# Two-layer hybrid trunk on one core: six more ring slots for the experts' weights, in memory that attention, caches, filter and retention no longer need

## The reference

```
for l in range(2):
    mod = silu(cond) @ w_ada[l] + b_ada[l]                  # six parts: sh1, sc1, g1, sh2, sc2, g2
    h = rms_norm(x, norm1) * (1 + sc1) + sh1
    qa, ka, va, hy, qr, kr, vr, gr = split(h @ w_in[l])
    ya = diff_attention(rope(qa), [k_cache, rope(ka)], [v_cache, va])   # caches and rope: latent group
    yb = hyena(hy)                                          # long convolution by FFT, implicit filter
    yc = rms_norm(retention(qr, kr, vr, s_cache)) * silu(gr)
    ga, gb, gc = split(sigmoid(h @ w_gate[l] + b_gate[l]))
    merged = ga*(ya @ w_branch_a) + gb*(yb @ w_branch_b) + gc*(yc @ w_branch_c)
    x = x + g1 * (merged @ w_out[l])
    h2 = rms_norm(x, norm2) * (1 + sc2) + sh2
    gate = top-2 of the experts of the top-1 group, by softmax(h2 @ w_router)     # 16 experts
    x = x + g2 * sum_e gate_e * ((silu(h2 @ w1_e) * (h2 @ w3_e)) @ w2_e)          # d_ff 512
y = rms_norm(x, final_g)            # and the context group's new keys, values, retention states
```

## Time and profile before

| | |
|---|---|
| median of the runs | 1264.77 us (3 runs, 1264.11 to 1270.05) |
| span of the profiled execution | 1267.2 us, 18560 instructions |
| TensorE matmul busy | 1228.1 us, 97% of the span, 7762 matmuls |
| TensorE weight load busy | 929.2 us (73%) |
| VectorE, ScalarE, GpSimd busy | 363.3 us (29%), 222.0 us (18%), 39.5 us (3%) |
| moved by the DMA engines | 362.06 MB, mean 286 GB/s over the span |
| chain that ended last | TensorE 86%, DMA 9% (experts' weights 7%, dense weights 2%) |
| mean granted clock of TensorE | 0.990 |

### The profile page before, as it was taken

How to read it: one execution, slowest core, us unless ns; L and a number is a source line. 1 busy time by engine, 2 the same in 40 slices (tenths; PEclk the granted TensorE clock), 3 DMA queues, 4 the chain that set the end, 5 groups by cost and what they waited for, 6 DMA issues and landing times.

```text
span 1267.2 us, 18560 instructions
## 1 busy us (share of the span) xinstructions
PE 1228.1 (97%) x7762; PEld 929.2 (73%) x7762; DVE 363.3 (29%) x917; ACT 222.0 (18%) x469; POOL 39.5 (3%) x80
## 2 busy tenths in 40 slices
PE   6999999999999999999999999999999999999996
PEld 5678888888897666666558888887888776666663
DVE  2441153134236111111233223423243611111113
ACT  2141013231030100111124101223202010000011
POOL 1001110000000000000000012000000000000000
PEclk9899999999989999999999999999999999999999
DMA  9779443424967999999976844343345599999992
GB/s 387 315 290 388 140 158 127 147 100 151 350 254 313 417 421 421 420 420 420 418 293 253 361 161 143 129 141 134 122 149 195 236 418 421 421 420 420 420 421 111
DMA packets 52601, 362.06 MB, mean 286 GB/s; under 512 B 6592, under 2 KB 6752, under 8 KB 9760
## 3 DMA queue, kind: packets, MB, share of 16 engines
q1 hardware_dynamic: 48672, 350.33, 69.3%
q0 software_dynamic: 3840, 10.47, 2.4%
HBM read 356.56 MB, written 2.64 MB: 283 GB/s over the span
## 4 chain that ended last, share of the span: by engine, by line
PE 86%; DMA 9%; DVE 2%; ACT 1%; issue 1%; SPq 0%; DVEq 0%; ACTq 0%
PE bank L713 24%; PE bank L1014 13%; PE bank L1050 9%; DMA ring<-in_experts 7%; PE bank L893 7%; PE bank L997 5%; PE bank L922 4%; PE bank L708 4%; PE bank L637 4%; PE bank L1092 3%; DMA ring<-in_weights 2%; PE bank L724 2%; PE bank L1029 1%; PE bank L973 1%; PE bank L697 1%
## 5 line engine op out<-in xcount | busy, mean ns | idle before, releaser
L713 PE MATMUL bank<-h,ring 128*128 128x256 f32 x1472 | 326.3, 380 | 0.0
L713 PEld LDWEIGHTS bank<-h,ring 128*128 128x128 f32 x1472 | 276.8, 190 | 40.9 <-issue 4.4
L1014 PE MATMUL bank<-ring,gates 128*64 128x256 f32 x2048 | 226.2, 380 | 8.0 <-DMA ring<-in_experts 4.3
L1014 PEld LDWEIGHTS bank<-ring,gates 128*64 128x64 f32 x2048 | 152.1, 137 | 79.7 <-issue 11.6
L1050 PE MATMUL bank<-ring,gates 128*64 128x512 f32 x512 | 113.4, 595 | 0.0
L1050 PEld LDWEIGHTS bank<-ring,gates 128*64 128x64 f32 x512 | 35.3, 137 | 66.7 <-issue 66.7
L997 PE MATMUL bank<-uc,gates 128*128 128x128 f32 x576 | 67.9, 276 | 0.1
L997 PEld LDWEIGHTS bank<-uc,gates 128*128 128x128 f32 x576 | 65.9, 192 | 0.7 <-DVE uc L1612 0.4
L1616 DVE SCALAR_TENSOR_TENSOR gates<-gates,bank 128x512 f32<-128x512 f32 (+1 forms) x18 | 11.8, 658 | 172.6 <-issue 161.3
L1092 PEld LDWEIGHTS bank<-gates,uc 128*128 128x128 f32 x256 | 47.3, 190 | 18.8 <-issue 13.0
L1092 PE MATMUL bank<-gates,uc 128*128 128x256 f32 x256 | 59.5, 386 | 0.0
(11 more groups left out here) (258 smaller groups left out, 1077.6 us busy)
## 6 DMA issues: line engine op xcount, KB each, us to landing
ring<-in_experts SPq DMA_DIRECT2D x204, 1024.0 KB, 11.7
ring<-in_weights SPq DMA_DIRECT2D x128, 1024.0 KB, 6.5
cst<-in_consts POOLq DMA_DIRECT2D x1, 1345.0 KB, 11.2
x<-in_x_in SPq DMA_DIRECT2D x1, 1024.0 KB, 5.0
sc<-in_s_cache POOLq DMA_DIRECT2D x2, 512.0 KB, 10.0
probs<-qk POOLq DMA_DIRECT2D x32, 32.0 KB, 3.0
va<-row_scratch POOLq DMA_DIRECT2D x2, 512.0 KB, 7.2
vr<-row_scratch POOLq DMA_DIRECT2D x2, 512.0 KB, 9.2
```

The source lines that it names most:

```text
L713: last = pe.matmul(bank[b][:, c * TOK:(c + 1) * TOK], w[:, k, c * P:(c + 1) * P], h[:, k, :], start=(k == 0), stop=(k == KT - 1))
L1014: last = pe.matmul(bank[b][64 * j:64 * j + 64, half * 256:half * 256 + 256], hgat[:, k, 64 * j:64 * j + 64], w[j][:, k, :], start=(k == 0) ...
```

## The change

Six slots, `lent`, are added for the experts' pieces alone, and thirteen tiles become views into them. `ring_table` now gives each piece the slot that has been free longest. It returns for each piece the count `USED` that `s_weights_used` must have reached. A lent slot counts as free from the end of the layer's last merge piece on. SyncE waits for `s_stores_read` once per layer, ahead of the experts. GpSimd's loads of layer 1's caches wait until TensorE has used the last piece of layer 0's experts. `rows_sb` moves to `arg`. By the new table the first six expert pieces of a layer wait for the end of the merge. Of those in the middle, each waits for the piece 14 places before. The first dense pieces of layer 1 wait for a count 11 below their own number (before: 7), and from the ninth on 7 again.

```diff
 SLOTS = 8
+LENT = 6
...
-    slot, count, filled = [], [], [0] * SLOTS
-    for n, piece in enumerate(pieces):
-        at = n if n < SLOTS else slot[pieces.index(done[n - SLOTS])]
+    gone = {piece: n + 1 for n, piece in enumerate(done)}
+    free, filled = [0] * (SLOTS + LENT), [0] * (SLOTS + LENT)
+    slot, count, used = [], [], []
+    for (kind, layer, _), c in pieces:
+        lent = range(SLOTS, SLOTS + LENT) if kind == "moe" else ()
+        since = {at: free[at] for at in range(SLOTS)}
+        since.update({at: max(free[at], END["merge", layer, 5]) for at in lent})
+        at = min(since, key=lambda n: (since[n], n))
         filled[at] += 1
         slot.append(at)
         count.append(filled[at])
-    return slot, count
+        used.append(since[at])
+        free[at] = gone[(kind, layer, _), c]
+    return slot, count, used
...
         ring = sb("ring", P, SLOTS, PIECE)
+        lent = sb("lent", P, LENT, PIECE)
...
-        qk = sb("qk", P, 8, TOK)
-        mix = sb("mix", P, 8, TOK)
+        def part(slot, at, n):
+            return lent[:, slot, at:at + n]
+
+        qk = part(0, 0, 2048).rearrange("p (a b) -> p a b", a=8)
+        mix = part(1, 0, 2048).rearrange("p (a b) -> p a b", a=8)
...
-        kc = sb("kc", P, H_A, SEQ)
-        vc = sb("vc", P, H_A * DV_A)
-        sc = sb("sc", P, H_C, 2, DV_C)
-        filt = sb("filt", P, 3, C_B)
+        kc = part(2, 0, 512).rearrange("p (a b) -> p a b", a=H_A)
+        vc = part(2, 512, 512)
+        sc = part(2, 1024, 1024).rearrange("p (a b c) -> p a b c", a=H_C, b=2)
+        filt = part(4, 0, 1536).rearrange("p (a b) -> p a b", a=3)
...
-        rows_sb = amixT[0:16, 0, 0:P]
+        rows_sb = arg[0:16, :]
...
+            def fetch(source):
+                nonlocal n
+                if USED[n]:
+
+                    sp.wait_ge(s_weights_used, USED[n])
+                slot = ring[:, SLOT[n], :] if SLOT[n] < SLOTS else lent[:, SLOT[n] - SLOTS, :]
+                sp.dma_start(slot, source).then_inc(s_weights_in[SLOT[n]], 16)
+                n += 1
...
                 if kind != "moe":
                     continue
+
+                sp.wait_ge(s_stores_read, layer + 1)
                 for p in range(PAIRS + 1):
...
                 if layer == 0:
                     pool.wait_ge(s_mod_ready, ada_at(0, 1) + 1)
+                else:
+
+                    pool.wait_ge(s_weights_used, END["moe", layer - 1, 0])
                 pool.dma_start(kc[:, :, :], k_cache[layer]).then_inc(s_cache_in, 16)
```

More of the change, by code:

```diff
@@ L117, in ring_table @@
         count.append(filled[at])
-    return slot, count
-SLOT, FILL = ring_table()
+        used.append(since[at])
+        free[at] = gone[(kind, layer, _), c]
+    return slot, count, used
+SLOT, FILL, USED = ring_table()
 ADA_ORDER = [item[1:] for item in PLAN if item[0] == "ada"]
@@ L363, in trunk_program @@
         s_vr_copied = sem("vr_copied")
-        s_weights_in = [sem(f"weights_in{slot}") for slot in range(SLOTS)]
+        s_weights_in = [sem(f"weights_in{slot}") for slot in range(SLOTS + LENT)]
         s_weights_used = sem("weights_used")
@@ L399, in trunk_program @@
         gr = mix[:, 4:8, :]
-        kc = sb("kc", P, H_A, SEQ)
-        vc = sb("vc", P, H_A * DV_A)
-        sc = sb("sc", P, H_C, 2, DV_C)
-        filt = sb("filt", P, 3, C_B)
+        kc = part(2, 0, 512).rearrange("p (a b) -> p a b", a=H_A)
+        vc = part(2, 512, 512)
+        sc = part(2, 1024, 1024).rearrange("p (a b c) -> p a b c", a=H_C, b=2)
+        filt = part(4, 0, 1536).rearrange("p (a b) -> p a b", a=3)
         zt = sb("zt", P, C_B)
-        ysp = sb("ysp", P, 2, C_B)
+        ysp = part(5, 0, 1024).rearrange("p (a b) -> p a b", a=2)
         tmp = sb("tmp", P, C_B)
-        attr = sb("attr", P, H_C, SEQ)
-        qx = sb("qx", P, 2, 2, SEQ)
+        attr = part(4, 1536, 512).rearrange("p (a b) -> p a b", a=H_C)
+        qx = part(5, 1024, 512).rearrange("p (a b c) -> p a b c", a=2, b=2)
         dsum = sb("dsum", P, H_C, SEQ)
[L410 to L413, removed]
+        xi = part(5, 1536, 512).rearrange("p (a b c) -> p a b c", a=2, b=2)
+        probs = part(3, 0, 1024).rearrange("p (a b c) -> p a b c", a=2, b=2)
+        amix = part(3, 1024, 512).rearrange("p (a b) -> p a b", a=2)
+        amixT = part(3, 1536, 512).rearrange("p (a b) -> p a b", a=2)
         osq = zt
@@ L506, in _ @@
             n = dense = 0
+            def fetch(source):
[5 more added lines that the diff above has]
+                n += 1
             for kind, layer, _ in PLAN:
                 for _ in range(0 if kind == "moe" else PLAN_PIECES[kind]):
[L509 to L514, removed]
+                    fetch(weights[dense, :, :])
                     dense += 1
@@ L524, in _ @@
                         for part in (0, 2, 1, 3):
[L525 to L529, removed]
+                            fetch(experts[layer, bass.ds(e, 1), part, :, :].rearrange("a p c -> (a p) c"))
                     todo += [(2 * p - 2 + c % 2, 4 + c // 2) for c in range(4)] if p else []
                     for e_, part in todo:
[L533 to L536, removed]
+                        fetch(experts[layer, e_, part])
                 for part in (4, 5):
[L538 to L541, removed]
+                    fetch(experts[layer, bass.ds(e, 1), part, :, :].rearrange("a p c -> (a p) c"))
             for c in range(4):
@@ L619, in piece @@
                 pe.wait_ge(s_weights_in[SLOT[n]], 16 * FILL[n])
-                return ring[:, SLOT[n], :].rearrange("p (k n) -> p k n", n=width)
+                slot = ring[:, SLOT[n], :] if SLOT[n] < SLOTS else lent[:, SLOT[n] - SLOTS, :]
+                return slot.rearrange("p (k n) -> p k n", n=width)
             def spin(b, n):
```

## The result

| | before | changed |
|---|---|---|
| median of the runs | 1265.31 us (7 runs, 1264.11 to 1270.05) | 1258.86 us (7 runs, 1256.06 to 1263.18) |
| ratio | | 0.9939, 95% interval 0.9913 to 0.9964 |
| profiled span | 1267.2 us | 1255.4 us |
| mean granted clock of the profiled execution | 0.990 | 0.994 |

By the medians the changed kernel is 6.5 us faster, 0.5%; by the ratio, 0.6% or 7.7 us. A second set of six runs on another occasion gave the same ratio, 0.9939 (0.9919 to 0.9958). The profiled spans are 11.8 us apart, which is more than the medians.

The account below looks back on a forecast made before the run. TensorE and the expert-weight transfers run nearly level, TensorE losing 5.9 us to stalls. Removing these takes the span from 1267.2 to 1261.3 us and the median from 1264.77 to 1258.9; forecast 1259.0, range 1255 to 1264.5.

Parts of the forecast that it names:

- The 5.9 us: TensorE's stalls for expert weights in both layers, 3.63 us in layer 1 and 2.25 in layer 0, all predicted to go.
- the steady 0.9 us per pair: In the experts, 12 weight pieces take 29.9 us against TensorE's 29.01 per pair, so transfers fall back 0.9 us.
- 14.9 us against 3.6: Six pieces of added lead, 14.9 us, against 3.6 us missing in layer 1's experts and 2.3 in layer 0's: no stall left.
- Steps costed at nothing: Other parts of the change, such as stores' wait, moved cache loads, dense pieces, row copy and views, each taken at zero.
- The stores' wait: SyncE's wait once per layer ahead of the experts' pieces: zero, as the signal comes before the merge's end.
- The cache loads: Layer 1's 1 MB of loads, moved to the end of layer 0's experts: zero, bounds minus 0 and plus 2.5 us.
- The rule on the transfer limit: A 358 GB/s limit between HBM and SBUF would make the experts' six slots worth about 35 us; the prediction followed the trace.
- The rival with fewer GB/s at 14 pieces outstanding: DMA engines move 10% less, 379 GB/s, in the experts, giving 1291 us; chance 0.05.
- The issue to landing: Time from a piece's issue to its landing, 11.7 us before, expected to stay about 12 us.
- The 2.4 us: Median 1264.77 us lay 2.4 us under the profiled span: elsewhere, giving 1258.9, or stalls of the profiled execution only, giving 1261.3.
- The clock: TensorE's half-speed clock in layer 1's narrow router matmuls and what follows: plus or minus 3 us, taken at zero.
- Half-clock stretches of another number: A sign in the changed kernel's profile that the prediction would be wrong: a different count of TensorE's half-clock stretches.

## Why the prediction was right

**The bound.** The reading that TensorE and the transfers run nearly level, and that full DMA slices say nothing of what slots are worth, was right. Half the bytes gain no more than six slots do.

**The size of the stalls.** The 5.9 us came out to the hundredth in the trace: 2.26 us in layer 0 and 3.63 in layer 1 are what the pairs of the changed kernel lack. Its source was read a little too simply: 1.7 us of it are two single late pieces, and the steady 0.9 us per pair accounts for the other 4.2.

**The lead.** The step "14.9 us against 3.6" held, with 13.8 to 14.6 us by the landing times. The lead is several times what is needed: two slots already leave no stall, and one leaves the computed 1.1 us, in part by chance, as a single piece that landed 1.0 us late is in it.

**Steps costed at nothing.** The stores' wait, the row copy, the dense pieces and the other views: with no slot lent the ratio is 1.0005, so together they are worth 1.4 us of gain or 2.7 us of cost at most. The cache loads were issued right at the end of layer 0's experts, and the swaps behind them 80 us later, as predicted:

```profile
639.59 0.53 POOL L587 DMA_DIRECT2D lent<-in_s_cache  x1
720.53 4.06 POOL L563 DMA_DIRECT2D lent<-lent  x8 [80.41 <-ACT lent L1402]
```

**The rule on the transfer limit.** The Trainium skill ("DMA: Bandwidth & Descriptors", "Where 436 GB/s comes from") puts the limit from HBM at some 358 GB/s. With one core in use, no full window here agrees: 423 GB/s for 20 us and more with the deeper queue. The rival with fewer GB/s at 14 pieces outstanding fell by the same rows.

**What was off.** The sum went by one profiled execution's stalls, and the forecast allowed for smaller ones in the runs. They are rather larger. The ratio stands for 7.7 us (4.6 to 11), and at a like clock the kernels are 6 to 8 us apart. The kernel with no slot lent shows how: single transfers that come late by some 1.5 us, which a kernel without lead pays at once and one with lead does not. Four more stores per layer point the same way: 19.1 us more stalls than the trace of before, but only 16 us more time than its runs, 17 at a like clock. That the average run of before has 7.5 to 8 us of stalls fits all of these, but no run shows it directly. The issue to landing was to stay at about 12 us and is 13.0 and 13.6 in the median. The six pieces that queue behind one another at the merge's end are not the reason: without the first 14 pieces of each layer the median is still 13.5 us, against 12.0 in before. Why it rose is not shown.

**The 2.4 us.** The prediction weighed what the 2.4 us between the profiled span and the median were. The two are not the same measure: in every run with both numbers the time is 1.7 to 1.9 us above the span, so a span of 1267.2 stands for some 1269.0, and 4.2 us were to be explained. The clock explains most of them: at the profiled execution's 0.990 the runs of before beside the experiments take 1266.5 to 1268.8 us. The sum was right all the same, since it took the stalls off the median.

**What was luck.** That 1258.86 lies 0.1 us from the forecast is chance. The base, 1264.77, was the median of three runs and became 1265.31 with seven and 1265.96 in the set after it, and runs of one kernel spread over some 7 us.

**The clock.** Taken at plus or minus 3 us for layer 1, it moved the pair of profiles by 6.1 us, over three places. Half-clock stretches of another number were named as a sign of being wrong, and they came; as they also differ between the two profiles of the changed kernel, they were no such sign. Had only the two spans been compared, the gain would have been taken for twice its size.

## What to carry to other kernels

A deeper ring is worth the stalls it removes, not its bytes: take the time per step from an undisturbed step and from the late ones, and compare their sum with the lead that the idle transfer time ahead of the stretch can buy. One or two slots may do what six do; the rest is insurance against late transfers, and here it carried 8 MB of foreign traffic for 1 to 3 us, most of them the clock's. Compare kernels over runs and per pair of steps, not by the spans of two profiles, when stretches at half the clock come and go between runs.

## What had not been expected of the hardware

In the profiles TensorE's granted clock fell to 1.2 GHz for 3.4 or 6.8 us at a time, at two to four places, differently in runs of one kernel, and some 5 us of the time went with it. In the kernel with no slot lent it also fell in the middle of the experts. At 1206.58 TensorE had stood still for 2.15 us; the next 32 matmuls took 5.33 us instead of 3.67, and the window reads:

```profile
1206.00:1210.00 4.00, 3.42 (x16) 2.18 (x18) 0.00 (x0) 0.00 (x0) 0.00 (x0) 0.57 1.01 422
```

So 1.7 us of slower clock followed this late transfer. It was seen once, and the 18 waits of up to 2.1 us in the kernel before with stores brought none, so that the wait brought it is not shown. A store of 1 MB from SBUF to HBM on a full queue delayed the loads by 2.4 us, about what a load of 1 MB takes (2.49 us): beside full loads it was not free.

Single pieces landed 0.5 to 1.6 us late in full stretches, once or twice per layer in each of eight profiles, each beside a load of instructions. Nine in ten of these loads have no late piece beside them.
